# Merge stage: the output product as three fp32r products on split operands, its inputs loaded in the stage before

## The reference

```
y  = concat([rms_norm(conv_out, g_out_conv), rms_norm(attn_out, g_out_attn)], -1) @ w_out   # 1024 -> 1024
x2 = x + gate * y
h2 = rms_norm(x2, ln2_g) * (1 + scale) + shift
logits = h2 @ w_route                      # 4 groups and 32 experts, top-1 group, then top-2 experts
```

## Time and profile before

| | us |
|---|---|
| median of 3 runs | 2102.85 (2100.62 to 2103.23) |
| profiled execution | 2097.65 |
| its span, first to last instruction | 2095.8 |
| merge stage, first DMA to the last of DVE | 1147.7 to 1359.0 |
| expert stage begins | 1367.0 |
| PE busy in the whole span | 1886.3 (90%) |
| DVE, ACT, POOL busy | 1287.0, 1072.8, 224.6 |

### The profile page before, as it was taken

The page is one execution under the profiler, slowest core; times in us unless marked ns, Lnnn a source line. Parts: engine busy times, 40 slices in busy tenths (PEclk is TensorE's granted clock), DMA queues, the critical chain, the costliest instruction groups (busy, mean ns, idle before and its releaser), DMA issues. The chain is left out here.

```text
span 2095.8 us, 27806 instructions
## 1 busy us (share of the span) xinstructions
PE 1886.3 (90%) x9998; PEld 1477.4 (70%) x9998; DVE 1287.0 (61%) x1988; ACT 1072.8 (51%) x1684; POOL 224.6 (11%) x203
## 2 busy tenths in 40 slices
PE   6899995999997899988786799689999999999956
PEld 2699775999995566777532355478888888888842
DVE  1533423454443455777542466579999888887936
ACT  5311112444434566777431221078778787776733
POOL 0100000000000123333120000011000000000002
PEclk9999997999996999999998899789999999999987
DMA  8320125744214437121162822189999999999928
GB/s 300 87 101 33 51 82 183 254 164 164 91 42 140 136 96 216 24 90 28 28 247 89 314 106 95 51 313 425 426 421 417 410 413 419 417 413 371 393 104 323
DMA packets 155224, 444.19 MB, mean 212 GB/s; under 512 B 37178, under 2 KB 82046, under 8 KB 123298
## 3 DMA queue, kind: packets, MB, share of 16 engines
q1 hardware_dynamic: 136148, 341.04, 43.6%
q0 software_dynamic: 13792, 82.95, 10.3%
q10 hardware_dynamic: 5184, 18.88, 2.2%
HBM read 388.32 MB, written 58.70 MB: 213 GB/s over the span
## 5 line engine op out<-in xcount | busy, mean ns | idle before, releaser
L2824 DVE TENSOR_TENSOR moe_lo<-wts_raw,moe_hi 128x2048 fp32r<-128x2048 f32 x216 | 484.8, 2287 | 70.9 <-ACT moe_hi L2721 70.2
L2721 ACT ACTIVATE moe_hi<-wts_raw 128x2048 fp32r<-128x2048 f32 x216 | 402.1, 1915 | 51.8 <-PE moe_U L2602 25.3
L949 DVE TENSOR_TENSOR cmp_xl<-cmp_bank,cmp_xh 128x512 fp32r<-128x512 f32 (+1 forms) x136 | 82.6, 667 | 120.0 <-ACT cmp_xh L903 120.0
L1419 POOL TENSOR_SCALAR att_prow<-att_prow,att_scale 128x640 f32<-128x640 f32 (+15 forms) x96 | 113.6, 1197 | 370.2 <-DVE att_scale L1554 370.2
L873 PE MATMUL cmp_hp<-cmp_xh,cmp_wh 128*128 128x256 f32 (+2 forms) x512 | 150.5, 294 | 0.0
L873 PE MATMUL cmp_hp<-cmp_xh,cmp_wl 128*128 128x256 f32 (+2 forms) x512 | 146.7, 287 | 0.0
L873 PE MATMUL cmp_hp<-cmp_xl,cmp_wh 128*128 128x256 f32 (+2 forms) x512 | 146.5, 286 | 0.0
L1527 DVE TENSOR_TENSOR att_pl<-att_pT,att_ph 128x512 fp32r<-128x512 f32 (+5 forms) x148 | 101.2, 688 | 72.3 <-ACT att_ph L1453 71.9
L2022 POOL DMA_INDIRECT rou_xg<-s_h,rou_idx x36 | 50.0, 1389 | 800.9 <-PE moe_XT L2607 510.6
L1463 ACT ACTIVATE att_prow<-att_S,att_low 128x640 f32<-128x640 f32 (+15 forms) x192 | 107.5, 560 | 41.3 <-DVE att_low L1542 37.8
L2628 PE MATMUL moe_Y<-moe_hi,moe_hh 128*128 128x512 f32 x288 | 113.6, 394 | 10.9 <-DVE moe_hl L2844 7.9
(11 more groups left out here) (451 smaller groups left out, 4351.9 us busy)
## 6 DMA issues: line engine op xcount, KB each, us to landing
wts_raw<-in_w_gate SPq DMA_DIRECT2D x72, 1024.0 KB, 7.0
wts_raw<-in_w_up SPq DMA_DIRECT2D x72, 1024.0 KB, 7.6
wts_raw<-in_w_down SPq DMA_DIRECT2D x72, 1024.0 KB, 8.7
s_yb<-moe_y ACTq DMA_DIRECT2D x36, 512.0 KB, 8.1
smi_kvs<-in_w_ada SPq DMA_DIRECT2D x8, 2048.0 KB, 8.3
fro_wraw<-in_w_ada SPq DMA_DIRECT2D x4, 2048.0 KB, 11.8
s_yb<-att_zero SPq DMA_DIRECT2D x1, 8192.0 KB, 33.1
fro_wraw<-in_w_in SPq DMA_DIRECT2D x12, 512.0 KB, 5.5
```

The source lines that it names most:

```text
L1419: last = pool.tensor_scalar(row, row, scale[:, grp, h:h + 1], None, ALU.mult)
L2721: act.activation(hi[p][half][:, :], raw[p][half][:, :], ACT.Copy).then_inc(hi_ready[p], 1)
L2824: dve.tensor_tensor(lo[p][half][:, :], raw[p][half][:, :], hi[p][half][:, :], ALU.subtract).then_inc(lo_ready[p], 1)
```

## The change

The output product is made of split operands, as the expert stage does it already: `wh` is `w_out` times the gain of its channel, rounded to fp32r (ACT), `wl` the rest (DVE); `ch`, `cl` the same for a conv tile (ACT, POOL) and `ah`, `al` for an attention tile (ACT, DVE). The product is high x high, high x low and low x high. The conv tile is not scaled; instead the attention rows are scaled by the ratio of the two roots, and Y is scaled by the reciprocal conv root when it is read. The conv output is loaded tile by tile, squared on POOL and summed on PE into a column of `M`. `MergeAhead` loads the gains, `w_out` (into the buffers of the expert weights), two conv tiles and one attention tile in the sample stage; prompt tile 0 now comes first and the 8 sample rows second. In the tile loop the router product comes a tile later than before, as do `place` and, on DVE, the logits.

```diff
         def _(sp):
+            ahead.load(nc, a, sp)
             sp.wait_ge(done, 1)
...
+class MergeAhead:
+
+    SEQ = [0, TT - 1] + list(range(1, TT - 1))
+
+    def __init__(self, s, rt, weights):
+        self.rt, self.weights = rt, weights
+        self.conv = [rt.xg[0][:, i * CW:(i + 1) * CW].rearrange("p (j n) -> p j n", j=CJ) for i in range(2)]
+        self.attn = [rt.xg[1][:, i * CW:(i + 1) * CW] for i in range(2)]
+        self.gcol = s.sb("gcol", [P, 2, CJ])
+        self.row_in = s.sem("row_in")
+        self.gain_in = s.sem("gain_in")
+        self.conv_in = [s.sem(f"conv_in{i}") for i in range(2)]
+        self.attn_in = [s.sem(f"attn_in{i}") for i in range(2)]
+        self.wo_in = [s.sem(f"wo_in{i}") for i in range(4)]
+
+    def wo(self, k):
+
+        return self.weights.raw[k // 4][k % 4 // 2][:, k % 2 * D:(k % 2 + 1) * D]
+
+    def load_conv(self, nc, a, sp, i):
+        t = self.SEQ[i]
+        n = rows_of(t)
+        with nc.allow_non_contiguous_dma(reason="columns of a few rows"):
+            sp.dma_start(self.conv[i % 2][:, :, 0:n], a["s_convT"][:, :, t * P:t * P + n].rearrange("j p n -> p j n")
+                         ).then_inc(self.conv_in[i % 2], 16)
+
+    def load_attn(self, a, sp, i):
+        t = self.SEQ[i]
+        n = rows_of(t)
+        sp.dma_start(self.attn[i % 2][0:n, :], a["s_attn"][t * P:t * P + n, :]).then_inc(self.attn_in[i % 2], 16)
+
+    def load(self, nc, a, sp):
+        with nc.allow_non_contiguous_dma(reason="gains by channel"):
+            sp.dma_start(self.gcol[:, 0, :], a["g_out_conv"][0].rearrange("(j p) -> p j", p=P)).then_inc(self.gain_in, 16)
+            sp.dma_start(self.gcol[:, 1, :], a["g_out_attn"][0].rearrange("(j p) -> p j", p=P)).then_inc(self.gain_in, 16)
+        self.load_conv(nc, a, sp, 0)
+        self.load_attn(a, sp, 0)
+        sp.dma_start(self.rt.ident[:, :], a["c_ident"]).then_inc(self.row_in, 16)
+        sp.dma_start(self.rt.ones[:, :], a["c_ones"]).then_inc(self.row_in, 16)
+        for q in range(4):
+            sp.dma_start(self.weights.raw[q // 2][q % 2].rearrange("p (k n) -> p k n", k=2),
+                         a["w_out"][0, q * 2 * P:(q + 1) * 2 * P].rearrange("(k p) n -> p k n", p=P)).then_inc(self.wo_in[q], 16)
+        self.load_conv(nc, a, sp, 1)
...
+            ahead.load_attn(a, sp, 1)
             load_x(0)
-            load_attn(1)
...
+            for h in range(2):
+                weights.load(sp, weights.DOWN, h, 0)
+
+            for p in range(2):
                 for h in range(2):
+                    k = 4 * p + 2 * h + 2
+                    sp.wait_ge(wh_ready, k)
+                    sp.wait_ge(wl_ready, k)
                     weights.load(sp, p, h, 0)
             for i, t in enumerate(seq):
                 n = rows_of(t)
                 if i + 2 < TT:
+                    sp.wait_ge(ch_ready, i + 1)
+                    sp.wait_ge(cl_ready, i + 1)
+                    sp.wait_ge(sq_ready, i + 1)
+                    ahead.load_conv(nc, a, sp, i + 2)
                     sp.wait_ge(turned, i + 1)
-                    load_attn(i + 2)
+                    ahead.load_attn(a, sp, i + 2)
                 sp.wait_ge(h2_ready, i + 1)
                 sp.dma_start(a["s_x2"][t * P:t * P + n, :], x2[i % 2][0:n, :]).then_inc(x2_out[i % 2], 16)
                 sp.dma_start(a["s_h2"][t * P:t * P + n, :], h2[i % 2][0:n, :]).then_inc(x2_out[i % 2], 16)
                 if i + 2 < TT:
                     load_x(i + 2)
...
         def _(pool):
+            for i, t in enumerate(seq):
+                n = rows_of(t)
+                c = conv[i % 2][:, :, 0:n]
+                pool.wait_ge(conv_in[i % 2], 16 * (i // 2 + 1))
+                pool.wait_ge(sq_sum, i)
+                pool.tensor_tensor(sq[:, :, 0:n], c, c, ALU.mult).then_inc(sq_ready, 1)
+                pool.wait_ge(ch_ready, i + 1)
+                if i >= 2:
+                    pool.wait_ge(product, i - 1)
+                pool.tensor_tensor(cl[i % 2][:, :, 0:n], c, ch[i % 2][:, :, 0:n], ALU.subtract).then_inc(cl_ready, 1)
...
+            high_conv(0)
+            high_weights(0)
             root(0)
-            for k, part in enumerate(parts):
-                act.wait_ge(sq_sum, k + 1)
-                act.activation(crow[:, part], sums[k], ACT.Sqrt, bias=eps[:, :], scale=1.0 / CW).then_inc(conv_roots, 1)
-                if k == 1:
-                    scale(0)
+            conv_root(0)
+            high_weights(1)
+            high_weights(2)
+            scale(0)
+            high_weights(3)
+            high_conv(1)
+            high_attn(0)
+            for k in range(4, KT):
+                high_weights(k)
+            root(1)
+            conv_root(1)
+            scale(1)
+            high_attn(1)
             for i, t in enumerate(seq):
                 n = rows_of(t)
                 st = stat[:, t, :]
-                if i + 1 < TT:
-                    root(i + 1)
-                    scale(i + 1)
+                if i + 2 < TT:
+                    conv_root(i + 2)
                 act.wait_ge(x2_ready, i + 1)
-                step(act.activation(junk[0:n, :], x2[i % 2][0:n, :], ACT.Square, accum_out=st[0:n, 3:4]))
-                act.activation(st[0:n, 4:5], st[0:n, 3:4], ACT.Sqrt, bias=eps[0:n, :], scale=1.0 / D).then_inc(root2, 1)
+                step(act.activation(h2[i % 2][0:n, :], x2[i % 2][0:n, :], ACT.Square, accum_out=st[0:n, 6:7]))
+                act.activation(st[0:n, 7:8], st[0:n, 6:7], ACT.Sqrt, bias=eps[0:n, :], scale=1.0 / D).then_inc(root2, 1)
+                if i + 2 < TT:
+                    high_conv(i + 2)
+                    root(i + 2)
+                    scale(i + 2)
+                    high_attn(i + 2)
...
+            def sum_squares(i):
+
+                n = rows_of(seq[i])
+                pe.wait_ge(sq_ready, i + 1)
+                if i:
+                    pe.wait_ge(conv_roots, i)
+                if i >= 4:
+                    pe.wait_ge(logits_read, i - 3)
+                for j in range(CJ):
+                    last = pe.matmul(M[0:n, i % 2:i % 2 + 1], sq[:, j, 0:n], ones[:, 0:1], start=(j == 0), stop=(j == CJ - 1))
+                last.then_inc(sq_sum, 1)
+
+            def products(i, high, low, k, start, stop):
+
+                n = rows_of(seq[i])
+                for x, w, first, final in ((high, wh, start, False), (high, wl, False, False), (low, wh, False, stop)):
+                    for c in range(2):
+                        last = pe.matmul(Y[i % 2][c][0:n, :], x[:, k % CJ, 0:n], w[:, k, c * 512:(c + 1) * 512],
+                                         start=first, stop=final)
+                return last
 
             pe.wait_ge(row_in, 32)
-            for k, part in enumerate(parts):
-                pe.wait_ge(sq_ready, k + 1)
-                for j in range(CJ):
-                    last = pe.matmul(sums[k], ones[:, :], sq[:, j, part], start=(j == 0), stop=(j == CJ - 1))
-                last.then_inc(sq_sum, 1)
+            sum_squares(0)
             for i, t in enumerate(seq):
-                n = rows_of(t)
-                if i < 3:
-                    pe.wait_ge(cT_ready, i + 1)
-                if i == 0:
-                    pe.wait_ge(wo_in[0], 16)
-                if i == 1:
-                    pe.wait_ge(conv_roots, 3)
+                pe.wait_ge(ch_ready, i + 1)
+                pe.wait_ge(cl_ready, i + 1)
                 if i >= 2:
                     pe.wait_ge(y_read, i - 1)
                 for j in range(CJ):
-                    for c in range(2):
-                        pe.matmul(Y[i % 2][c][0:n, :], cT[:, j, t * P:t * P + n], wo[:, j, c * 512:(c + 1) * 512], start=(j == 0), stop=False)
-                    if j == 1:
-                        turn_attn(i)
-                    if j == CJ - 1 and i:
+                    if i == 0:
+                        pe.wait_ge(wh_ready, j + 1)
+                        pe.wait_ge(wl_ready, j + 1)
+                    products(i, ch[i % 2], cl[i % 2], j, j == 0, False)
+                    if i == 0 and j == 0:
+                        pe.wait_ge(const_in, 16 * NCONST)
+                    if i == 0 and j == 0:
+                        sum_squares(1)
+                    if j == 0 and i >= 2:
+                        pe.wait_ge(conv_roots, min(i + 2, TT))
+                        route(i - 2)
+                    if j == 1 and i >= 3:
+                        pe.wait_ge(logits_read, i - 1)
+                        place(i - 3)
+                if i == 0:
+                    turn_attn(0)
+                pe.wait_ge(ah_ready, i + 1)
+                pe.wait_ge(al_ready, i + 1)
+                for j in range(CJ):
+                    if i == 0:
+                        pe.wait_ge(wh_ready, CJ + j + 1)
+                        pe.wait_ge(wl_ready, CJ + j + 1)
+                    last = products(i, ah[i % 2], al[i % 2], CJ + j, False, j == CJ - 1)
+                    if j == 0 and i >= 3:
```

(63 more changed lines are left out.)

182 lines of the change are left out of this document (88 added, 94 removed).

## The result

The changed kernel takes **2166.07 us**, median of 4 runs (2163.26 to 2166.47), against 2101.73 us for the kernel before in the same measurement (2099.34 to 2103.23): a ratio of 1.0304, 95% interval 1.0286 to 1.0322, slower. Its profiled execution took 2165.72 us, with a span of 2163.9 and a mean granted clock of 0.928 (0.950 before).

The account below looks back on a forecast made before the run. PE bounded the merge stage before; the change makes a serial ring through the conv load. 1200 + 24.9 + 22.6 + 4 x 27.2 + 15.6 + 15.0 + 27.9 = 1414.8 against 1358.95, +56 us: 2159 us, range 2122 to 2186.

Parts of the forecast that it names:

- The bound of before: Merge stage of the kernel before: PE sets the pace, 18.4 us a tile, with nothing else close.
- the ring: Merge tiles: product, h2, stores, conv load, POOL square, column sums, next product, all in series; 27.2 us per full tile.
- Its terms: Steps of a full tile: h2 ready at 10.0, load landed at 16.8, square 1.6, column sums to Y read 8.8 us.
- Tiles 1, 2, 7 and 8: Merge tiles unlike the full ones: 24.9 and 22.6 us; the last two, which sum nothing, 15.6 and 15.0.
- The start: Head of the merge stage: constants, splits and conv tile 2 hold tile 0, done at about 1200 us; stage opens at 1147.7.
- The tail: End of the merge stage, after the last product: 27.9 us, 2.8 more than before.
- The clock: PE restarting at the 1.2 GHz level after idling ahead of the column sums: 2.1 us a tile.
- The product: PE's output product: 48 fp32r matmuls take 10.9 us a tile instead of 13.7, 2.8 us less.
- Outside the merge stage: Sample and expert stages: early loads costed at nothing, expert stage starting as before.
- Its own sign of being wrong: Sample stage: the forecast is wrong if this stage gets longer; the early loads there were costed at nothing.
- the one with PE as the bound: Rival for the merge stage: conv tile arrives in time, PE never waits for sums, 15.6 us a tile; 2083 us, chance 0.09.

Follow-up runs that it names:

- e1: Changed kernel with the load of conv tile i+3 issued on SP ahead of the wait for h2 of tile i instead of behind it; 2099.3 us.
- e12: Changed kernel with four more squares of each conv tile on POOL, into a spare tile, ahead of the square that counts; 2188.4 us.
- e4: Changed kernel with the early loads issued at the head of the merge stage instead of in the sample stage; 2181.8 us.
- e7: Changed kernel with 17 unused float32 matmuls in the place of PE's idle time ahead of the column sums; 2152.8 us.
- e11: On e9, one float32 matmul in the place of each triple of fp32r matmuls in the output product; 2087.4 us.
- e5: On e1, three edits at the stage's head: later PE wait for constants, earlier load of conv tile 2, reordered splits on ACT and DVE; 2080.4 us.
- e10: On e9, without the third product (low activations by high weights), 32 fp32r matmuls a tile instead of 48, less exact; 2062.3 us.
- e9: On e5, attention tile 2 and conv tile 3 issued on SP ahead of the 6 MB of expert weights instead of behind them; 2072.1 us.

## Why the prediction was right, point by point

It said 2159 us, range 2122 to 2186, slower at 0.87; it is 2166.07.

- **The bound of before and the ring:** right, and shown from both sides by e1 (cut: -66.8 us) and e12 (lengthened: +4.67 us a period for 4.47 of work). The wait it named (PE for POOL's square, that for the load, SP for h2) is the one in the waits: PE idles 9.7, 8.4, 8.5 and 8.6 us ahead of the sums in tiles 3 to 6, where it had said some 9. One reading of it was too simple: in the kernel before, DVE waits for PE not once in a tile but four times, 0.69, 1.19 and 0.49 us beside the 3.42; nothing in the sum hung on it.
- **Its terms**, for a full tile: h2 ready at 10.0, measured 9.94 (1309.34 to 1319.28); load landed at 16.8, measured 16.91; square 1.6, measured 1.04; from the sums to the next Y read 8.8 (0.9 + 4.1 + 0.6 + 1.1 + 2.1), measured 9.35, since the sums themselves run at the lower level (1.86). Period 27.2, measured 27.35 to 27.54. Two sizes were off by half a microsecond each and cancelled, which is luck. I took the square from the scaling of 1.565 us, which was the wrong row for it. From the figure of the Trainium skill (GPSIMD Engine Reference, "Performance versus the Vector engine": 4497 ns for an addition of 2048 elements) I had worked out an estimate of 1.1 us, with which the measured 1.04 agrees.
- **Tiles 1, 2, 7 and 8:** 24.9, 22.6, 15.6, 15.0; measured 25.66, 23.67, 15.18, 14.74. The two first are 0.8 and 1.1 us longer than said; from their sums to the next Y read it is 9.2 and 9.6 us, not 8.8.
- **The start:** 52.3 us, measured 51.8, by the steps that it named, counted from the stage's start: PE back from the constants at 20.7 (said 22.3), conv tile 2 landed at 41.4 (said 42.7), and 10.4 us from there to the Y read (said 9.6), the clock lower behind the wait. The sizes again cancel in part. But its sentence that the early loads buy nothing as long as the constants come late is wrong: e4 shows them worth 12.5 us in this very kernel, because without them SP gets to those constants 12.9 us later. What is right is that the start still lost against the old one.
- **The tail:** 27.9, measured 27.9.
- **The clock:** 2.1 us, by e7 1.9.
- **The product:** 2.8 us a tile, by e11 2.55, with the matmuls 0.234 us apart and not 0.227.
- **Outside the merge stage:** costed at nothing. Its own sign of being wrong, a longer sample stage, stands in the first pair of profiles (116.3 against 114.6 us), but the twelve profiles with the same loads go from 114.5 to 117.5 and e4 without them has 117.5. The stage took 57.5 us more in the profiles (said 56), the medians 64.3 more. Of the 6.8 left, the barrier behind the stage took 0.5 in the profiles (8.8 against 8.3 us). For the rest no mechanism was found: over the 13 profiles, the change of the median less the change of the stage (both against before) goes from -4 to +9 us, +3 on average, for kernels with the same code outside but for e4's early loads. That is the size of the differences between profiles of unchanged stages; whether a small part is due to the placement of tiles stays open.
- **The rivals:** the one with PE as the bound (2083) needed the load ahead of the h2 stores. e1 made that true and got periods of 16.1, where it had 15.6; its time was only reached with the head mended as well (e5: 2080).

## What to carry to other kernels

A prefetch that sits on one in-order queue behind stores which wait for results is not a prefetch: it becomes a ring through the previous tile, and its length, and not the work of the busiest engine, sets the period. Look where each load stands in its queue and what the waits ahead of it need; moving the conv load past the wait for h2 was worth 66.8 us of 2166. The same at a stage's start: put the few small transfers that the next tile needs ahead of the megabytes for the stage after (18 us from issue to landing in e5), and wait for constants where they are read.

## What the runs showed of the hardware that I had not expected

- A conv tile of 256 KB released its reader 3.07 us after its issue when it went first, 5.23 us behind two stores and a residual load, and 17 to 18 us behind 6 MB of expert weights: what was issued ahead of it set its arrival.
- PE's idle time alone did not tell the clock behind it. After 3.1 us of waiting in the head of the changed kernel (1181.4 to 1184.5) its matmuls still came 0.23 us apart, with a granted clock of 0.97 from 1181 to 1190; in e10 the sums at 1198.29, after 2.6 us of waiting, took 1.87 us, with a granted clock of 0.61 from 1197 to 1201. Two waits of the same length parted as well: behind 2.05 us in e1 (to 1213.99) the attention transposes took 0.60 us, behind 2.11 in e9 (to 1185.73) 1.05. I know no row that tells them apart.
- Two loads of the router's weights and bias held SP for 2.7 and 4.2 us in the issue alone (changed kernel, 1159.60 and 1162.37); 9.97 us for the first in the kernel before. Everything behind them on the queue is later by as much.
- POOL's square of a 128x512 tile took 1.04 us in the ring of the changed kernel, where DVE was idle, and 2.04 to 2.10 us three times in e9 (1164.38, 1183.59, 1200.73), where DVE was at work on operations of 512 and 1024 columns. With only smaller DVE operations beside it, it took 1.04 to 1.24. No run changes this alone, so that DVE is the cause isn't shown.
